# Who multiplies the level masks: moving 24 small products of a blockwise inversion from GpSimd to VectorE

## The reference

```python
lower = jnp.where(strict, jnp.einsum('bhnid,bhnjd->bhnij', kb, k) * gamma, 0.0)
tmat = lower + jnp.eye(C, dtype=lower.dtype)
u = solve(v * beta[..., None])            # triangular_solve with tmat
w = solve(kb * jnp.exp(g)[..., None])
qk = jnp.einsum('bhnid,bhnjd->bhnij', q, k) * gamma

def step(S, inp):
    q_i, k_i, u_i, w_i, g_i, qk_i = inp
    v_new = u_i - jnp.einsum('bhcd,bhde->bhce', w_i, S)
    o = (jnp.einsum('bhcd,bhde->bhce', q_i * jnp.exp(g_i)[..., None], S)
         + jnp.einsum('bhij,bhje->bhie', qk_i, v_new))
    S = (S * jnp.exp(g_last)[..., None]
         + jnp.einsum('bhcd,bhce->bhde', k_i * jnp.exp(g_last - g_i)[..., None], v_new))
    return S, o
```

## Time and profile before

| | |
|---|---|
| median of three executions | 2004.63 us (2002.62 to 2005.17) |
| the profiled execution | 2004.85 us, of which its span 2003.2 us |
| PE / DVE / ACT / POOL busy | 1980.1 / 1290.0 / 747.9 / 109.4 us |
| mean granted TensorE clock | 0.999 |
| the two inversions | about 609.4 to 645 us and 672.8 to 709 us of the span |

### The profile page before, as it was taken

The page is one execution under the profiler, slowest core; times in us unless marked ns, Lnnn a source line. Parts: engine busy times, 40 slices in busy tenths (PEclk is TensorE's granted clock), DMA queues, the critical chain, the costliest instruction groups (busy, mean ns, idle before and its releaser), DMA issues.

```text
span 2003.2 us, 27276 instructions
## 1 busy us (share of the span) xinstructions
PE 1980.1 (99%) x10235; PEld 1677.3 (84%) x10237; DVE 1290.0 (64%) x1810; ACT 747.9 (37%) x977; POOL 109.4 (5%) x166
## 2 busy tenths in 40 slices
PE   9999999999999999999999999999999999999998
PEld 7888888897789989888888988888888888888887
DVE  6877577775758875877677753363246642567676
ACT  5321222344564434322222333212235432645553
POOL 1010010000003300100001000000000000000000
PEclk9999999999999999999999999999999999999999
DMA  9555455622110003655555532342234422144553
GB/s 355 173 195 181 165 199 168 200 95 85 64 53 21 1 22 106 210 184 180 176 193 166 171 127 91 103 171 98 82 108 151 164 100 89 43 180 149 186 173 121
DMA packets 51450, 275.30 MB, mean 137 GB/s; under 512 B 6081, under 2 KB 6401, under 8 KB 31649
## 3 DMA queue, kind: packets, MB, share of 16 engines
q1 hardware_dynamic: 31536, 203.71, 28.9%
q0 software_dynamic: 19104, 69.41, 10.5%
q10 hardware_dynamic: 720, 0.95, 0.2%
HBM read 272.99 MB, written 1.05 MB: 137 GB/s over the span
## 4 chain that ended last, share of the span: by engine, by line
PE 92%; DVE 4%; ACT 3%; issue 1%; ACTq 0%; DVEq 0%
PE ps L1178 15%; PE ps L1180 15%; PE ps L1179 15%; PE ps L1415 6%; PE ps L1413 6%; PE ps L1414 6%; PE ps L1190 6%; PE ps L1191 3%; PE ps L2729 2%; PE ps L2730 2%; PE ps L2731 2%; PE ps L2242 1%; DVE w_lo L775 1%; PE ps L2254 1%; PE ps L2815 1%
## 5 line engine op out<-in xcount | busy, mean ns | idle before, releaser
L1178 PE MATMUL ps<-h_parts,w_lo 128*128 128x512 f32 (+1 forms) x1424 | 538.5, 378 | 2.7 <-DVE h_parts L1046 1.3
L1180 PE MATMUL ps<-h_parts,w_hi 128*128 128x512 f32 (+1 forms) x1424 | 534.4, 375 | 0.0
L1179 PE MATMUL ps<-h_parts,w_hi 128*128 128x512 f32 (+1 forms) x1424 | 534.2, 375 | 0.0
L775 DVE TENSOR_TENSOR w_lo<-w_raw,w_hi 128x2048 fp32r<-128x2048 f32 (+3 forms) x189 | 392.5, 2077 | 184.2 <-ACT w_hi L507 184.1
L507 ACT ACTIVATE w_hi<-w_raw 128x2048 fp32r<-128x2048 f32 (+3 forms) x191 | 331.9, 1738 | 418.8 <-PE ps L1415 254.1
L783 DVE SCALAR_TENSOR_TENSOR ada_product<-ada_w,silu_c 128x1024 bf16<-128x1024 f32 x256 | 313.2, 1223 | 20.3 <-DVE ada_product L783 10.1
L1178 PEld LDWEIGHTS ps<-h_parts,w_lo 128*128 128x128 f32 x1424 | 268.3, 188 | 52.1 <-DVE w_lo L775 1.6
L1180 PEld LDWEIGHTS ps<-h_parts,w_hi 128*128 128x128 f32 x1424 | 268.1, 188 | 48.6
L1179 PEld LDWEIGHTS ps<-h_parts,w_hi 128*128 128x128 f32 x1424 | 268.4, 188 | 47.0
L519 ACT ACTIVATE sil<-ps 128x512 f32<-128x512 f32 x66 | 39.5, 598 | 481.2 <-PE ps L1180 481.2
L1414 PE MATMUL ps<-hid_parts,w_hi 128*128 128x512 f32 x468 | 182.2, 389 | 0.0
(11 more groups left out here) (371 smaller groups left out, 2595.2 us busy)
## 6 DMA issues: line engine op xcount, KB each, us to landing
w_raw<-in_w_up SPq DMA_DIRECT2D x88, 1024.0 KB, 4.8
ada_w<-in_ada POOLq DMA_DIRECT2D x128, 512.0 KB, 3.6
w_raw<-in_w_down SPq DMA_DIRECT2D x24, 768.0 KB, 4.2
w_raw<-in_w_ret_t SPq DMA_DIRECT2D x16, 1024.0 KB, 4.8
w_raw<-in_w_down SPq DMA_DIRECT2D x24, 640.0 KB, 3.9
w_raw<-in_w_ab SPq DMA_DIRECT2D x14, 1024.0 KB, 4.8
w_raw<-in_w_down SPq DMA_DIRECT2D x9, 1024.0 KB, 4.8
ada<-in_ada SPq DMA_DIRECT2D x8, 1024.0 KB, 22.3
```

Of the source, the lines that this page charges most:

```text
L775: dve.tensor_tensor(w_lo[parts_of(s, slot)][:, 0:elems], raw_of(s, slot)[:, 0:elems], w_hi[parts_of(s, slot)][:, 0:elems].bitcast(F32), AL ...
L1178: pe.matmul(out, lo, rhs_hi(k), start=first and k == 0, stop=False)
L1179: pe.matmul(out, hi, rhs_lo(k), start=False, stop=False)
L1180: mm = pe.matmul(out, hi, rhs_hi(k), start=False, stop=last and k == nk - 1)
```

## The change

`pool_deltanet` is gone, and GpSimd goes from one loop of weight tiles straight into the next. VectorE makes M_1 to M_6 of both chunks itself, with the same operands and the same outputs:

```diff
@@ pool_program
-        pool_deltanet(pool)
@@
-    def pool_deltanet(pool):
-        for s in range(2):
-            for l in range(1, LEVELS):
-                for c in range(2):
-                    if l < 3:
-                        inv(pool, iv_dve, INV_DVE, c, s, ("SYS", "T0")[l - 1])
-                    else:
-                        inv(pool, iv_pe, INV_PE, c, s, f"X{l - 1}")
-                    pool.tensor_tensor((xb if l == 1 else cut)[c][:], coup[c][:], over(levels[:, l * P:(l + 1) * P], 4), ALU.mult) \
-                        .then_inc(iv_pool[c], 1)
@@ cross
-            inv(pe, iv_pool, INV_POOL, c, s, f"M{l}")
+            inv(pe, iv_mask, INV_MASK, c, s, f"M{l}")
@@ coupled, behind M_0
+            masked(c, 1)
+
+        def masked(c, l):
+            dve.tensor_tensor((xb if l == 1 else cut)[c][:], coup[c][:], over(levels[:, l * P:(l + 1) * P], 4), ALU.mult) \
+               .then_inc(iv_mask[c], 1)
@@ begun, behind T_0
+            inv(dve, iv_dve, INV_DVE, c, s, "T0")
+            masked(c, 2)
@@ the loop over levels
         for l in range(1, LEVELS - 1):
             for c in range(2):
                 tt = 2 * s + c
+                if l >= 2:
+                    inv(dve, iv_pe, INV_PE, c, s, f"X{l}")
+                    masked(c, l + 1)
                 inv(dve, iv_pe, INV_PE, c, s, f"C{l}")
```

More of the change, by code:

```diff
@@ L2101, in build @@
                       "N3", "T3", "KE", "N4", "T4", "N5", "T5", "KD", "T6"])
-    INV_POOL = stages([f"M{l}" for l in range(1, LEVELS)])
-    iv_pool = [sem(f"dn_masked{c}") for c in range(2)]
+    INV_MASK = stages([f"M{l}" for l in range(1, LEVELS)])
+    iv_mask = [sem(f"dn_masked{c}") for c in range(2)]
     RUNS = [(s, b) for s in range(2) for b in range(2)]
```

## The result

The changed kernel takes 2008.89 us (median of 11 runs), the kernel before 2004.8 in the same comparison. The ratio is 1.0023 with a 95% interval of 1.0016 to 1.0031: 4.6 us slower, between 3.2 and 6.2 (the two medians lie 4.1 apart). The forecast was 4.9 us. In the profiled executions the span went from 2003.2 to 2006.7 us.

A forecast was written before the change was run, and what follows sets the result against it. Up to N_4(0) a loop through DVE and PE was taken to bound the levels, behind it PE alone. 0.77 + 1.70 and 0.67 + 1.72, together 4.9 us, on 2004.85 gave 2009.7, less 0.2: 2009.5; range 2007.0 to 2012.2.

The forecast's parts named there:

- The price of a mask: Each mask product moved to DVE costs 0.61 us from start to start; 12 per inversion, 7.3 us in all.
- What GpSimd held up: Four DVE instructions of the first inversion, lengthened beside POOL masks, get back 3.2 us in all.
- The head: From M_0(0) to N_1(0): N_1(0) comes 0.77 us late in the first inversion, 0.67 in the second.
- The levels: N_1(0) to N_4(0): a loop through both engines takes 6.08 us per level, adding 1.70 and 1.72 us per inversion.
- Levels 4 to 6 and the rest: Behind N_4(0) the remaining masks fit into DVE's waits, adding nothing; outside the inversions nothing changes either.
- The sum: Both inversions: 2.5 and 2.4 us, together 4.9 us more, giving 2009.5 us; chance 0.60.
- slower: Whole kernel: a time from 2008.6 us up, as 4.0 us can be told from no change; chance 0.69.
- The covered masks: Up to N_4(0), DVE's idle time and time given back hide the added masks: 2003.7 us, not slower; chance 0.08.
- The queue rival: In the levels only DVE's queue counts: lags of 2.06 and 1.96 us, together 4.0, 2008.6 us; chance 0.15.
- The granted clock: PE's new waits make its clock fall once in each inversion, adding 3.4 us: 2012.9 us; chance 0.08.
- the first rival: The covered masks: bringing the masks back to DVE might cost nothing, 2003.7 us; chance 0.08.

## Why the prediction was right

*The price of a mask.* The 24 instructions take 0.68 to 0.69 us, and 0.61 from start to start in a full queue, as their twin M_0 did.

*What GpSimd held up.* All four long instructions are at 0.68 to 0.69, 1.09 to 1.10 and 1.22 us. The run without masks adds that of these 3.2 us the path of the kernel before had only 1.1 to 1.4.

*The head.* Foreseen lags 0.77 and 0.67 us, measured 0.73 and 0.63. N_0(1) came 0.40 late, as reckoned (0.41). T_0(1) followed it after 0.92 us and not after 0.95 as before, which is most of the difference.

*The levels.* Foreseen three distances of 6.08 us, measured 6.07, 6.08 and 6.07. That a loop through both engines bounds and not VectorE's queue (5.9) was argued from the links and is now shown by three kernels: a product more in the loop costs 0.61, the same product outside it 0.39, and the mask moved into a wait costs 0.3 less until the queue of 5.87 takes over. In a fourth, with the loop shortened by its side product, TensorE's 5.42 takes over.

The prediction doesn't say why the middle distance was 5.60 us before, and not 5.47. There VectorE's queue bounded, made longer by GpSimd: `q_grown` took 2.15 us, so T_2(1) started 1.22 us behind P_2(1), and not 1.09 as T_1(1) did. The two starts, in the timelines of PE and DVE of the kernel before:

```profile
627.43 1.06 PE L2254 MATMUL ps<-turned,xbuf 128*128 128x128 f32 x8
628.65 0.67 DVE L2465 TENSOR_TENSOR inv_t<-inv_t,ps 128x512 f32<-128x512 f32 x1
```

The sum used the measured distance, so this did not touch it.

*Levels 4 to 6 and the rest.* From N_4(1) to T_6(1) it is 10.88 us in both kernels (638.70 to 649.58, 640.63 to 651.51). GpSimd's next DMA again waited for a dot product of VectorE, now for 391 us.

*The sum.* 4.9 foreseen, 4.7 in the traces, 4.6 timed. Unrounded, 4.86 us were foreseen and the traces show 4.74, and 0.08 of the difference are the two heads. The timing is less sure than the traces: its interval begins at 3.2 us, below the 4.0 us from which the prediction speaks of "slower", the case to which it gave 0.69. That the kernel lost time is shown; that it lost more than 4.0 us is shown only by the inversions in the traces.

*The rivals.* The covered masks failed at the point named: N_4(0) comes 28.8 us behind M_0(0), not 26.4. Their idea is right in another kernel, the one with the side products spread and M_2 moved: there M_1(1) and M_2(0) stand in a wait of VectorE, and M_3 to M_6 in levels that TensorE bounds. The queue rival was off by 0.4 us per inversion. The granted clock did not fall further: over the first inversion it is 0.96, over the second 1.00, both as before, although PE is idle for 3.7 and 4.3 us in them. The windows of the changed kernel (stretch, its length, busy time and count of PE, PEld, DVE, ACT and POOL, clock, DMA share, GB/s):

```profile
608.97:651.50 42.53, 38.80 (x317) 37.45 (x316) 37.59 (x54) 17.85 (x28) 0.00 (x0) 0.96 0.00 1
674.80:717.10 42.30, 38.04 (x326) 36.78 (x325) 38.09 (x54) 21.95 (x34) 0.00 (x0) 1.00 0.01 1
```

The sentence on offloading between the two engines (the Trainium skill, page "Perfetto Trace Analysis", section "Optimizing Scalar/DVE Operations") says that such a move might not help. Turned round, as the first rival took it, it does not hold for this change, which costs 4.7 us. What they give each other back is real (3.2 us of instruction time per inversion), but whether it counts is decided by where the instructions stand.

## What to carry to other kernels

Where two engines hand work to each other in turns, write down the loop link by link from start to start and compare it with each engine's own queue; the longest of the three is the pace, and an instruction costs its full time only in the longest. Read the pace on the engine that never waits: while TensorE went at 5.42 us, VectorE's distances were 4.95, 5.85 and 4.98. A delay in the loop passed on in full here (N_4(0) and T_6(1) both came 2.41 us later), while a gain stopped at TensorE's own pace (1.1 us at N_4(0), 0.3 at the end). An idle share of 17% hides nothing if it lies behind the part that is bound. Before moving work onto an engine, look for the places where it waits, put the work there, and take out of the loop what need not be in it.

## What the runs showed of the hardware

A VectorE instruction with two SBUF inputs that starts inside a GpSimd instruction that reads SBUF ends 0.55 us behind the end of that one, for a 128x512 product that takes 0.68 alone (610.14). The `q_grown` product of 1.22 us started 0.20 us behind a mask and took 2.15. Such a mask takes 1.27 us when nothing holds it up, in POOL's timeline of the kernel before:

```profile
617.26 1.27 POOL L2179 TENSOR_TENSOR cut<-coup,levels 128x512 f32<-128x512 f32 x1
```

In the kernel with spread side products and GpSimd's masks, where less of the mask was left, it took 1.56, in DVE's timeline:

```profile
626.52 1.56 DVE L2451 TENSOR_TENSOR q_grown<-dn,grown 128x1024 f32<-128x1024 f32 x1
```

So it is the rest of the other's instruction that is waited for, and not a slower rate. The Trainium skill says the same of the shared port pair (page "SBUF — State Buffer", section "Who interferes with whom"); that GpSimd's products are held up in turn shows in the 1.78 us of the one at 609.50, which started 0.05 us behind VectorE's M_0(0). The products N and T, with one input in PSUM, keep 0.67 to 0.68 us beside a GpSimd mask, for example N_2(1) in the timeline of the kernel with only the head's masks on VectorE, while GpSimd's pair of masks runs from 625.77 to 629.26:

```profile
628.05 0.67 DVE L2466 TENSOR_TENSOR inv<-inv,ps 128x512 f32<-128x512 f32 x1
```
